# Attention of the first block: mask and maximum in one VectorE operation, division by the sum on ScalarE one head later

## The reference, cut to what matters

```
score = sum_h relu(qi_h . ki) * wi_h          # index scores of 8 heads, causal
idx   = top_k(score, 128)                     # 128 keys stay for each query
s     = (q_h . k_sel) * 64 ** -0.5            # 8 heads, 2 groups of keys and values
s     = where(valid, s, -inf)
p     = softmax(s)                            # exp(s - max) / sum
o     = p . v_sel
```

## Time and profile before

| | us |
|---|---|
| median of 3 runs (3137.0 to 3139.91) | 3138.04 |
| span of the profiled execution, first to last instruction | 3140.3 |
| TensorE matmul busy in that span | 2816.1 (90%) |
| VectorE busy | 1862.0 (59%) |
| ScalarE busy | 1153.1 (37%) |
| GpSimd busy | 1024.6 (33%) |

### The profile page before, as it was taken

One profiled execution on the slowest core, in us unless ns is written; L12 is line 12 of the kernel. 1 busy time (PEld: TensorE's weight loads), 2 busy tenths in 40 slices (PEclk: granted clock), 3 DMA queues, 4 the chain that ended last, 5 costly groups with the idle time before them and its releaser, 6 DMA issues. The chain is left out here.

```text
span 3140.3 us, 59087 instructions
## 1 busy us (share of the span) xinstructions
PE 2816.1 (90%) x25000; PEld 2221.6 (71%) x25000; DVE 1862.0 (59%) x2779; ACT 1153.1 (37%) x2127; POOL 1024.6 (33%) x582
## 2 busy tenths in 40 slices
PE   7999798999989998999999799978888887699987
PEld 5765476877867655767778587857777775479975
DVE  6878765886059786478840456456666654353062
ACT  4334434333242344243321512234555533242252
POOL 1422132444424221334444222244444430132202
PEclk9989899999999999999999899989999987899988
DMA  6322133433323211244332323220000003033111
GB/s 214 95 74 54 33 90 100 142 114 91 98 81 89 74 47 48 81 129 144 118 89 86 122 79 101 85 74 15 12 23 24 24 8 139 29 111 91 54 38 54
DMA packets 350230, 249.42 MB, mean 79 GB/s; under 512 B 10874, under 2 KB 322448, under 8 KB 349456
## 3 DMA queue, kind: packets, MB, share of 16 engines
q1 hardware_dynamic: 342704, 229.62, 24.3%
q10 hardware_dynamic: 7264, 16.03, 1.6%
HBM read 221.59 MB, written 16.52 MB: 76 GB/s over the span
## 5 line engine op out<-in xcount | busy, mean ns | idle before, releaser
L540 POOL TENSOR_TENSOR weights_lo<-weights_raw,weights_hi 128x1024 fp32r<-128x1024 f32 (+2 forms) x230 | 582.7, 2534 | 1115.1 <-ACT weights_hi L509 1115.1
L1181 PE MATMUL psum<-moving_hi,weights_hi 128*128 128x512 f32 x1472 | 602.9, 410 | 40.5 <-PEq L178 13.6
L1181 PE MATMUL psum<-moving_lo,weights_hi 128*128 128x512 f32 x1472 | 582.8, 396 | 0.0
L1181 PE MATMUL psum<-moving_hi,weights_lo 128*128 128x512 f32 x1472 | 582.3, 396 | 0.0
L1181 PEld LDWEIGHTS psum<-moving_hi,weights_hi 128*128 128x128 f32 x1472 | 281.6, 191 | 161.6 <-issue 68.5
L509 ACT ACTIVATE weights_hi<-weights_raw 128x1024 fp32r<-128x1024 f32 (+1 forms) x240 | 248.3, 1036 | 249.8 <-PE psum L1181 245.0
L1181 PEld LDWEIGHTS psum<-moving_hi,weights_lo 128*128 128x128 f32 x1472 | 281.8, 191 | 61.1
L1181 PEld LDWEIGHTS psum<-moving_lo,weights_hi 128*128 128x128 f32 x1472 | 282.6, 192 | 56.4 <-issue 3.8
L2598 POOL TENSOR_TENSOR second_off<-second_mats,second_masks 128x256 f32<-128x256 f32 x180 | 141.6, 791 | 154.0 <-PE psum L2061 153.3
L2654 PE MATMUL psum<-hn_hi,even_hi 128*128 128x256 f32 x480 | 166.4, 347 | 8.6 <-DVE hn_lo L1998 7.7
L2654 PE MATMUL psum<-hn_lo,even_hi 128*128 128x256 f32 x480 | 164.1, 342 | 0.0
(11 more groups left out here) (470 smaller groups left out, 6136.1 us busy)
## 6 DMA issues: line engine op xcount, KB each, us to landing
weights_raw<-in_w_up SPq DMA_DIRECT2D x88, 512.0 KB, 3.8
weights_raw<-in_w_in SPq DMA_DIRECT2D x80, 512.0 KB, 3.6
ada<-in_ada_w SPq DMA_DIRECT2D x9, 2048.0 KB, 8.9
odd_raw<-in_od_w_in SPq DMA_DIRECT2D x16, 1024.0 KB, 5.5
even_raw<-in_ev_w_in SPq DMA_DIRECT2D x30, 512.0 KB, 4.0
weights_raw<-in_w_down SPq DMA_DIRECT2D x32, 448.0 KB, 3.6
weights_raw<-in_w_o SPq DMA_DIRECT2D x16, 512.0 KB, 3.9
weights_raw<-in_w_down SPq DMA_DIRECT2D x16, 512.0 KB, 3.9
```

Of the source, the lines that this page charges most:

```text
L540: ops.tensor_tensor(self.ring.lo[i % n][:, a:b], self.ring.raw[:, t % self.ring.landing, a:b], self.ring.hi[i % n][:, a:b].bitcast(F32), A ...
L1181: return nc.tensor.matmul(to, (hi, lo)[which][:, at:at + P], moving(k)[part], start=start and k == 0 and i == 0, stop=stop and k == n_k - ...
```

## The change

`peak` becomes one instruction: VectorE adds the mask to the scores, multiplies by -1/8 and keeps the minimum of the row as accumulated output. It gives the negated scores and, as their minimum, the negated maximum. `exp` turns the sign back with scale -1. The semaphore `max_ready` goes; `exp` waits on `scores_taken`. `norm` is split: VectorE does only the reciprocal (`invert`), at place h + 1 of a head in place of h + 2, and ScalarE multiplies the row by it, behind the next head's `exp` and ahead of `take`.

```
-                    nc.vector.scalar_tensor_tensor(prob[:, h, 0:S], score_bank(n, S), HEAD_DIM ** -0.5, left_out[:, 0:S],
-                                                   ALU.mult, ALU.add).then_inc(scores_taken, 1)
-                    dve.wait_ge(scores_taken, n + 1)
-                    nc.vector.tensor_reduce(stat[:, 0, h:h + 1], prob[:, h, 0:S], AX_X, ALU.max, negate=True)\
-                        .then_inc(max_ready, 1)
-                def norm(b, h):
-                    S = (b + 1) * P
+                    nc.vector.tensor_tensor_reduce(out=prob[:, h, 0:S], in0=score_bank(n, S), in1=left_out[:, 0:S], scale=-HEAD_DIM ** -0.5,
+                                                   scalar=3.0e38, op0=ALU.add, op1=ALU.min, accum_out=stat[:, 0, h:h + 1])\
+                        .then_inc(scores_taken, 1)
+                def invert(b, h):
                     dve.wait_ge(exp_ready, b * HEADS + h + 1)
-                    chain.then(nc.vector.reciprocal(stat[:, 2, h:h + 1], stat[:, 1, h:h + 1]))
-                    nc.vector.tensor_scalar(prob[:, h, 0:S], prob[:, h, 0:S], stat[:, 2, h:h + 1], None, ALU.mult)\
-                        .then_inc(normed, 1)
+                    nc.vector.reciprocal(stat[:, 2, h:h + 1], stat[:, 1, h:h + 1]).then_inc(inverted, 1)
...
-                        if h >= 2:
-                            norm(b, h - 2)
+                        if 1 <= h <= HEADS:
+                            invert(b, h - 1)
...
                 def exp(b, h):
-                    act.wait_ge(max_ready, b * HEADS + h + 1)
+                    act.wait_ge(scores_taken, b * HEADS + h + 1)
                     x = prob[:, h, 0:(b + 1) * P]
-                    nc.scalar.activation(x, x, ACT.Exp, bias=stat[:, 0, h:h + 1], accum_out=stat[:, 1, h:h + 1])\
+                    nc.scalar.activation(x, x, ACT.Exp, bias=stat[:, 0, h:h + 1], scale=-1.0, accum_out=stat[:, 1, h:h + 1])\
                         .then_inc(exp_ready, 1)
+                def norm(b, h):
+                    act.wait_ge(inverted, b * HEADS + h + 1)
+                    x = prob[:, h, 0:(b + 1) * P]
+                    nc.scalar.activation(x, x, ACT.Identity, scale=stat[:, 2, h:h + 1]).then_inc(normed, 1)
...
                         exp(b, h)
+                    if 1 <= h <= HEADS:
+                        norm(b, h - 1)
                     if h >= 3:
                         take(b, h - 3)
```

More of the change, by code:

```diff
@@ L975, in attention @@
         stat = sb("stat", [P, 3, HEADS])
-        names = ("logits_ready logits_taken weighted step scores_ready scores_taken max_ready "
-                 "exp_ready normed turned turned_taken pv_ready o_taken")
+        names = ("logits_ready logits_taken weighted step scores_ready scores_taken "
+                 "exp_ready inverted normed turned turned_taken pv_ready o_taken")
         places = [(b, h) for b in range(QB) for h in [-1] * (b > 0) + list(range(HEADS + 3))]
@@ L986, in attention @@
             s = Products(nc, sems, ring, loads, groups, psum, [(4 * 512, 512), (5 * 512, 512)], ahead=ahead)
-            (logits_ready, logits_taken, weighted, step, scores_ready, scores_taken, max_ready,
-             exp_ready, normed, turned, turned_taken, pv_ready, o_taken) = s.more
+            (logits_ready, logits_taken, weighted, step, scores_ready, scores_taken,
+             exp_ready, inverted, normed, turned, turned_taken, pv_ready, o_taken) = s.more
             bank = lambda b, n=512: psum[:, b * 512:b * 512 + n]
```

## The result

The changed kernel takes 3148.65 us (median of 13 executions, 3140.79 to 3156.32), the kernel before 3139.91 in the same 13 rounds. The ratio of the times is 1.0021, 95% interval 1.0011 to 1.0031: slower by 3 to 10 us, right at what can be told from no change. The forecast was 3142.1, +0.13%, with a range to 3149: the median lies 0.35 us inside that range, and above the 3138 to 3145 that the forecast gave for its own mechanism alone.

What follows compares the result with a forecast made beforehand. TensorE was taken to set the pace, its idle time in attention being what counts. Later copies in the drains, +3.2 us, and clock, +0.9, gave +4.1 on 3138.0: 3142.1 us, range 3132 to 3149.

Steps and rivals of the forecast that it cites:

- its own mechanism: Attention drains: ScalarE's copy out of the transpose bank comes late, clock about as before; 3138 to 3145 us, chance 0.58.
- What bounds the kernel: Attention stages: TensorE's idle time counts, not VectorE's load; in block 2 TensorE already sets the pace at 2.28 us.
- The cap on what a faster VectorE can give: Both layers' attention: TensorE's waits for VectorE's multiplication, 4.2 + 2.7 = 6.9 us, unless something else moves with it.
- Mask and maximum in one: VectorE, block 2: two slots of 1.05 us become one of 0.7; worth nothing on TensorE's path in blocks 0, 2, 3.
- The multiplication on ScalarE: ScalarE multiplies in 0.51 us at 384 keys, 0.40 at 256; its work still fits, 1.97 us against 2.28 in block 2.
- The new wait and the round: Block 2: loop of relu, weighing, reciprocal, multiplication and copy through both engines takes 2.35 us per head against TensorE's 2.28.
- The drains: Ends of attention blocks, per layer: block 0 +0.3, block 1 +0.7, block 2 +0.6, block 3 0; both layers +3.2 us.
- The clock: First layer's block 1 drain: granted clock may fall as in the second's, 1.9 us at one in two, taken as +0.9.
- VectorE was the bound, and its waits go: Rival, attention: TensorE's waits for the multiplication vanish, at most 6.9 us, to 3131 or about 3128; chance 0.14.
- The clock falls longer: Rival, second layer's attention opening: fall lasts 17.0 us like the first's, not 6.4; +5.3, to 3147.4 us; chance 0.23.
- Not at one pass: Rival, blocks 1 to 3: fused instruction takes 2.1 us, costing some 29 us, to 3170; chance 0.05.

Runs made afterwards that it cites:

- the best order without filled drains: Fused mask and maximum, with the whole division on VectorE one place earlier and ahead of the weighing, against the kernel before: ratio 0.9973, -4.5 us at equal clock.

## Why the prediction was right, point by point

The forecast had the cause, the sign and the size of the part that it worked out, the order of the two engines. That the measured median stayed inside the range is in part luck: it lies only 0.35 us under the upper end, and of the 6.6 us that the ratio stands for the order accounts for 3.8.

- *What bounds the kernel.* Right. VectorE lost 48.5 us of work and the program got slower. The cap on what a faster VectorE can give, 6.9 us, held at equal clock: the fused operation alone gave 3.9, the best order without filled drains 4.5. The cap said "unless something else moves with it"; with the reciprocal first the clock did, and gave more than the cap.
- *Mask and maximum in one.* Priced at 0.7 us, between 0.55 and 1.05. It took a slot of 0.47 (315.99 to 316.46) and 0.08 for the read-out, 0.55 in all: no more than the masking alone, and under the price. That it would be worth nothing on TensorE's path was wrong for block 2. TensorE waited there for the multiplication at 314.80, 0.61 us, and at 317.04, 0.27, which the forecast's "without a wait", read from two turns of the middle, passed over. Alone the new operation took 0.98 us off block 2's drain, and 0.57 us inside the new order.
- *The multiplication on ScalarE.* Priced at 0.51 at 384 keys; its slot is 316.63 - 316.11 = 0.52. The rule of the Trainium skill that speaks against it ("ScalarE: Activation LUTs", "Rules for kernel authors") came out on the right side here, but not for the reason of its price: with the reciprocal early the multiplication on ScalarE costs nothing that shows (21.90 against 21.85 us in block 2 with it on VectorE, and within the intervals at equal clock).
- *The new wait and the round.* 2.35 us a head forecast, 2.37 measured. On TensorE it doesn't show at every head, as I had it ("block 2's turns are 2.3 us or more apart"): up to head 3 they stay at its own 2.28, and the whole loss of block 2 comes at heads 4 and 5, which followed in 1.79 and 2.24 us before and in 2.31 and 2.37 now. The sum came out because the copy of head 4 is as late as forecast. This is the step that decided, and two experiments that each move one call show it: with either the copy or the reciprocal put first, the loss at equal clock is gone (-0.6 and -2.8 us for +3.8), with the same instructions on the same engines.
- *The drains.* Block 0 +0.3 forecast, +0.34 measured; block 1 +0.7, measured 20.82 - 20.04 = +0.78; block 2 +0.6, measured +0.64 in the first layer; block 3 0, measured 0.01. Sum +3.2 for both layers against 3.5 of the drains and 3.8 +- 1.2 of the fit. In block 1 the turn of head 5 was to come at 273.96, 18.88 us behind the block's first scores; it came 1126.95 - 1108.07 = 18.88 us behind them in the second layer.
- *The clock.* Not settled. I took 0.9 us; the two mean clocks, 0.9450 and 0.9442, are worth 1.9 +- 2.9, so that neither the 0.9 nor nothing at all is ruled out. In the profiled pair TensorE's time at 0.50 in the two stages went from 54.6 to 68.3 us, but it grew by 16.7 us outside them as well. The falls behind block 2 went from 6.8 to 10.2 us in both layers, and the first layer's block 1, which had none, got one of 13.6, where I had put one like the second layer's at one in two and looked for nothing longer; the first layer's opening fall went from 17.1 to 10.2.
- *The rivals.* "VectorE was the bound, and its waits go" falls for this change and holds in part for half of it: with the fused operation alone the waits for the multiplication went from 6.9 us to 3.6 in both layers together, and 3.9 us were gained at equal clock. "The clock falls longer" was placed at the wrong spot. The second layer's opening fall stayed at 6.8 us; the longer stretches lie behind the drains, which I had changed. "Not at one pass" falls with the 0.54 us row.

The order on ScalarE and VectorE is shown as the cause of the 3.8 us. That TensorE's gaps in the drains of blocks 0 and 2 cause the falls behind them is shown by filling them. Which gap brings a fall of what length, and why the reciprocal first alone has a higher mean clock than any other kernel without filled drains, stays open. So does whether the change moves the clock at all: executions of the changed kernel had mean clocks from 0.941 to 0.947, those of the old one from 0.939 to 0.949.

## What to carry to other kernels

When an operation moves to another engine, write down both engines' orders and follow one round: what it waits for there, what that waits for, and what is queued behind it. Here both engines had room, yet together they were slower than the one had been, and moving a single call ahead of another turned a loss of 0.2% into a gain of 0.4%, some 7 us of it at equal clock. Where TensorE sets the pace, its short gaps can cost more than their length, since the granted clock fell behind many of them here; the cheapest 0.7% in this kernel was unrelated matrix work put into the gaps, and it came without any change to the attention.

## What the runs showed of the hardware

- A VectorE operation with an accumulated minimum, one source in PSUM and one in SBUF, takes as long as the plain one (0.54 us at 384 columns against 0.55); reading out the accumulator is an instruction of its own of 74 to 85 ns.
- Gaps of TensorE of 0.5 to 1.9 us, several within the drain of a block, were enough for the granted clock to go to 0.50, the 1.2 GHz level, for 3.4 to 13.6 us. They weren't sure to: behind the same last gap of 1.39 us in block 2 the clock fell in the changed kernel and stayed at 1.00 with the reciprocal first. With the gaps of blocks 0 and 2 filled, no fall was left there in five profiled executions.
- Each 0.001 of mean clock was worth 2.4 us of 3140 in the fit over all kernels, so the changed kernel, whose clock varied from 0.941 to 0.947, varied by 15 us, more than the change under test. Drain times read from the profile repeated to 0.03 us and told the orders apart where times of 12 executions didn't.
